# A hybrid decoder layer: sampled-value products written to four groups of output partitions by page number

## What is computed

```python
k_past = cache_k[l, page_table].reshape(db, past, N_HEADS, HEAD_DIM)
v_past = cache_v[l, page_table].reshape(db, past, N_HEADS, HEAD_DIM)
s = einsum('bqhd,bkhd->bhqk', q, k) * HEAD_DIM ** -0.5 + c_q - c_k
p = softmax(s)
o = einsum('bhqk,bkhd->bqhd', p, v)
```

## Time and profile before

| what | value |
|---|---|
| median of 3 runs | 3033.57 us (3032.75 to 3034.82) |
| the profiled execution's own time | 3031.26 us |
| its span, first to last instruction | 3029.5 us |
| mean granted TensorE clock | 0.968 |
| TensorE matmuls busy | 2848.4 us (94%) |
| VectorE busy | 1490.4 us (49%) |
| ScalarE busy | 718.6 us (24%) |
| DMA moved | 516.15 MB, mean 170 GB/s |

### The profile page before, as it was taken

One profiled execution on the slowest core, in us unless ns is written; L12 is line 12 of the kernel. 1 busy time (PEld: TensorE's weight loads), 2 busy tenths in 40 slices (PEclk: granted clock), 3 DMA queues, 4 the chain that ended last, 5 costly groups with the idle time before them and its releaser, 6 DMA issues.

```text
span 3029.5 us, 51183 instructions
## 1 busy us (share of the span) xinstructions
PE 2848.4 (94%) x19952; PEld 2399.5 (79%) x19952; DVE 1490.4 (49%) x5784; ACT 718.6 (24%) x949; POOL 18.1 (1%) x57
## 2 busy tenths in 40 slices
PE   6977999999999977699899999999999999999998
PEld 4964546546545424499899999999999999999998
DVE  6367566566566347643534344343434344343433
ACT  5321101101101026622322222222222222222221
POOL 1000000000000000000000000000000000000000
PEclk8988999999999988799999999999999999999999
DMA  6468898898898863233132232223223222322321
GB/s 216 138 229 326 319 378 335 325 378 331 331 378 328 314 208 105 82 98 113 56 112 84 84 111 85 84 96 101 84 84 110 86 84 95 101 84 84 109 87 60
DMA packets 265863, 516.15 MB, mean 170 GB/s; under 512 B 14162, under 2 KB 171435, under 8 KB 265076
## 3 DMA queue, kind: packets, MB, share of 16 engines
q1 hardware_dynamic: 257828, 496.26, 46.0%
q10 hardware_dynamic: 5760, 10.49, 0.9%
q0 software_dynamic: 2032, 6.13, 0.5%
HBM read 489.24 MB, written 24.02 MB: 169 GB/s over the span
## 4 chain that ended last, share of the span: by engine, by line
PE 58%; DVE 3%; ACT 2%; issue 1%; DVEq 0%; ACTq 0%
PE ps L624 57%; DVE t_work L1333 1%; PE ps L627 0%; DVE t_rmax L1650 0%; DVE t_aux L1590 0%; DVE t_aux L1333 0%; ACT t_aux L1196 0%; ACT L1196 0%; ACT L1198 0%; ACT t_aux L1198 0%; DVE t_work L342 0%; ACT t_work L1226 0%; DVE t_work L1598 0%; ACT t_wh L1021 0%; ACT L1061 0%
## 5 line engine op out<-in xcount | busy, mean ns | idle before, releaser
L624 PE MATMUL ps<-t_xh,t_wh 128*128 128x260 f32 x4608 | 943.4, 286 | 17.9 <-ACT t_work L1061 8.0
L624 PE MATMUL ps<-t_xh,t_wl 128*128 128x260 f32 x4608 | 934.5, 285 | 0.0
L624 PE MATMUL ps<-t_xl,t_wh 128*128 128x260 f32 x4608 | 933.3, 284 | 0.0
L1333 DVE TENSOR_TENSOR t_wl<-t_wraw,t_wh 128x1024 fp32r<-128x1024 f32 x376 | 459.8, 1224 | 867.6 <-ACT t_wh L1021 867.3
L1021 ACT ACTIVATE t_wh<-t_wraw 128x1024 fp32r<-128x1024 f32 x376 | 398.1, 1060 | 1907.0 <-PE ps L624 1906.0
L624 PEld LDWEIGHTS ps<-t_xh,t_wh 128*128 128x128 f32 x4608 | 717.0, 190 | 65.0 <-issue 44.3
L624 PEld LDWEIGHTS ps<-t_xh,t_wl 128*128 128x128 f32 x4608 | 716.8, 190 | 0.0
L624 PEld LDWEIGHTS ps<-t_xl,t_wh 128*128 128x128 f32 x4608 | 716.1, 190 | 0.0
L1459 DVE CUSTOM_DVE_ANT_0 t_work<-t_r,t_work 128x128 f32<-128x128 f32 x2048 | 455.1, 286 | 218.2 <-DMA t_r<-in_cache_k 205.2
L624 PE MATMUL ps<-t_r,t_pr 128*8 128x512 f32 x1024 | 456.3, 596 | 30.0 <-DMA t_r<-in_cache_v 28.7
L624 PEld LDWEIGHTS ps<-t_r,t_pr 128*8 128x8 f32 x1024 | 85.3, 90 | 354.7 <-issue 282.0
(11 more groups left out here) (186 smaller groups left out, 1057.1 us busy)
## 6 DMA issues: line engine op xcount, KB each, us to landing
t_r<-in_cache_k SPq DMA_DIRECT2D x256, 512.0 KB, 7.2
t_r<-in_cache_v SPq DMA_DIRECT2D x256, 512.0 KB, 6.8
t_wraw<-in_w_up SPq DMA_DIRECT2D x44, 2048.0 KB, 8.0
t_wraw<-in_w_down SPq DMA_DIRECT2D x22, 2048.0 KB, 7.9
t_wraw<-in_w_in SPq DMA_DIRECT2D x20, 2048.0 KB, 9.5
t_wraw<-in_w_o SPq DMA_DIRECT2D x8, 2048.0 KB, 9.9
scr_proj<-t_stg ACTq DMA_DIRECT2D x40, 256.0 KB, 3.9
t_aux<-scr_proj SPq DMA_DIRECT2D x12, 768.0 KB, 4.7
```

What stands on the lines that cost most here:

```text
L624: return pe.matmul(out, lhsT, rhs, start=start, stop=stop)
L1333: return dve.tensor_tensor(out, in0, in1, op)
```

## The change

Value page p is written to PSUM partitions 32 * (p % 4) to 32 * (p % 4) + 7 instead of always 0 to 7. Each of the four groups begins its own sum with its first page (p < 4) and ends it with its last (p >= 28). The order of the pages, chunks, waits and counts stays. At the end of a round ScalarE copies all 128 partitions, and the eight small matmuls take 128 rows instead of 8, against `quad`, a 128 by 8 array with a one wherever the partition is m modulo 32, so that the four groups are added there. VectorE makes `quad` and clears banks 4 and 5 once, before round 0; TensorE waits for that.

```diff
+        quad = sb("quad", [P, HEADS])
...
-        osb = work[0:HEADS, 7168:8192]
+        osb = work[:, 7168:8192]
...
-        o_rows, o_cols, o_kept = sems("o_rows_ready o_columns_full o_columns_kept")
+        o_rows, o_cols, o_kept, o_zero = sems("o_rows_ready o_columns_full o_columns_kept o_rows_zeroed")
...
             def value_page(r, p):
                 pe.wait_ge(v_loaded[p % RING], r * (16 * PAGES // RING) + 16 * (p // RING + 1))
+                lane = 32 * (p % 4)
                 for c in range(2):
-                    last = mm(ps[0:HEADS, 4 + c, :], pr[:, p, :], vring[:, p % RING, c * 512:(c + 1) * 512],
-                              p == 0, p == PAGES - 1)
+                    last = mm(ps[lane:lane + HEADS, 4 + c, :], pr[:, p, :], vring[:, p % RING, c * 512:(c + 1) * 512],
+                              p < 4, p >= PAGES - 4)
                 last.then_inc(v_used, 1)
...
                     for h in range(HEADS):
-                        last = mm(ps[:, 7, 144 + h:145 + h], osb[:, h * P:(h + 1) * P], ident[0:HEADS, h:h + 1])
+                        last = mm(ps[:, 7, 144 + h:145 + h], osb[:, h * P:(h + 1) * P], quad[:, h:h + 1])
...
             broadcast_q(0, 1)
+            pe.wait_ge(o_zero, 1)
             round_(0, True, True, False)
...
-                                copy(osb.rearrange("p (c n) -> p c n", c=2), ps[0:HEADS, 4:6, :]).then_inc(o_rows, 1)
+                                copy(osb.rearrange("p (c n) -> p c n", c=2), ps[:, 4:6, :]).then_inc(o_rows, 1)
...
             dve.wait_ge(e_kept, 4)
+            dve.tensor_reduce(quad[:, :], ident[:, :].rearrange("p (j m) -> p m j", j=4)[:, 0:HEADS, :], AX.X, ALU.add)
+            dve.memset(ps[:, 4:6, :], 0.0).then_inc(o_zero, 1)
```

## The result

The changed kernel takes 3014.96 us (median of 4 runs, 3011.51 to 3017.69) against 3034.2 us before: a ratio of 0.9936, 95% interval 0.9919 to 0.9953, or 19 us less. I had forecast 54 us less. The sign was right and the size was not: the time lies inside my wide range, but at little more than a third of the forecast gain, and outside the forecast's own range of 2965 to 3000.

A forecast was written before the change was run, and what follows sets the result against it. TensorE's matmuls were taken as the first limit, the DMA close behind. Seven rounds -48, round 8 -7, set-up +1.3 gave -54 us, so 2980 us; range 2957 to 3036, the forecast's own 2965 to 3000.

The forecast's parts named there:

- What bounded the kernel before: Rounds 1 to 7: TensorE first, busy 760.6 of 786.6 us, the DMA close behind at a share of 0.91.
- Overlap of the page matmuls: Value bursts: only neighbouring pages' last and first matmuls overlap, saving 10.7 us per round on TensorE if all pages have landed.
- 13 places of 16: Burst of four value pages, matmuls starting and ending in program order: 13 places in line instead of 16, 1.29 us less.
- What the landed pages allow: Bursts of five: fifth page lands about 4 us after issue, so some 0.8 of 1.72 us gained; 7.1 us per round altogether.
- overlap, but lateness eats it: Rival: fifth page lands 5 us or more after issue, bursts of five stay 8.7 us, clock falls; 3020 us, chance 0.06.
- Bursts of four: Three bursts of four value pages per round, each 1.29 us shorter.
- The DMA from the other side: DMA's round: floor 94.4 us, plus 1.4 for weight loads, plus a lull of 8 to 9; sum 104 to 106 us.
- the other sum: TensorE's side of a round: 3 x 1.29 + 4 x 0.8 = 7.1 us less; both sides agree on about 105.5 us.
- Round 8: Last round, value pages without keys: 7 us gained, bounds 2 and 10.
- Set-up and copies: Before round 0, quad and clear cost 1.3 us once; ScalarE's 128-row copy and the 128-row small matmuls cost zero.
- The clock: TensorE idling 5 to 10% more costs nothing; 14 us kept in the range for half speed at round ends.

The follow-up runs named there:

- ring5_before: A fifth value buffer added to the kernel before, without the groups: 3002.2 us, ratio 0.9903, rounds of 108.5 us.
- two_groups: The change with value pages alternating between two groups of partitions instead of four: 3013.62 us, ratio 0.9937, rounds of 109.1 us.
- ring5: The change with a fifth value buffer, in place of VectorE's scrap array: 2993.21 us, ratio 0.9871, rounds of 106.4 us.
- one_group: The change with every page on partitions 0 to 7 again, its other parts kept: 3037.65 us, ratio 1.0011 against the kernel before.
- half_groups: The change with a page's two halves in two groups, odd and even pages in two pairs of groups: 3018.57 us, ratio 0.9958.
- best_g2: The change with two groups by page, a fifth value buffer, earlier first weights, and set-up before the query wait: 2964.43 us, ratio 0.9781.
- early_w: The change with each round's first 2 MB weight load issued just ahead of the fifth key page: 3004.39 us, ratio 0.9912.

## Why the prediction was wrong

**What bounded the kernel before: right, and half the truth.** TensorE's line is the first limit: 108.5 us per round when never kept waiting (ring5_before). The second limit was to be the DMA's full rate. It was the ring, in the fourth and fifth bursts, and in the others the time at which the loads behind the lull and the weights are issued and land.

**Overlap of the page matmuls: the mechanism right, the size too small.** I had assumed program order and 13 places of 16. The rows show 1.92 us for 16, four side by side. This error was to the kernel's favour and did not matter, as two_groups shows: with half the overlap the time is the same.

**What the landed pages allow: the step that failed.** I had seen that the fifth page's buffer comes free only with the burst's first page, and then wrote that the page lands about 4 us after issue and that 0.8 us are gained per burst of five. In the burst shown it takes 5.07 us, and the burst is 9.0 us instead of 8.75: nothing is gained. From the earlier trace rows I had read "within 4.8 us" and taken 4, below my only evidence, where the row said no more than that it was hardly late. Over the rounds it is 4.9 us in the mean. With 5 us the chain of that step gives no gain for four bursts of seven, and by the table they gain 0.4 us per round together, where the term said 3.2. The chain is not all of it: ring5 shortens the fourth and fifth bursts but not the third and the sixth. The sixth took 12.6 us before, 3.6 of them waiting for pages, and I had counted it as one more burst of 8.75 us. I had "overlap, but lateness eats it", 3020 us, as the last rival, at a chance of 0.06. It is near the result partly by luck: it counts more for the bursts of four than they gave, and takes off 14 us for a clock that did not fall at the rounds' ends.

**Bursts of four.** I counted 1.29 us for each of three, 3.9 us per round; they gave 2.1 (table). The first gained 5.1 us and the second lost 5.4, since its first page comes behind the round's first weights and the lull. In the round shown TensorE waited 3.31 us for a page, and the next three took 7.58 us, with the clock at 0.66 from 605 to 613 us (the line of the windows above). The pages set that length and not the matmuls: in rounds 2 to 7 the burst ends 25.8 to 26.6 us after the exponentials, and in two_groups, where it starts 2.2 us later and has less to wait, 25.6 to 26.8 us. From the round's exponentials to the third burst it is 32.5 us in both kernels (621.09 less 588.59 after, 624.85 less 592.21 before, 32.6). What stayed is the last burst, 4.6 us instead of 7.0: three of its pages had landed, and it waits 0.7 us in the mean for the fourth.

**The DMA from the other side: the check that did not check.** I added the lull to the full rate and got 104 to 106 us, and took the agreement with the other sum as support. That sum assumed that the mid-round dips would go. ring5 has exactly that, with 106.4 us; the change has 296 and 274 GB/s in the dips and 109.7 us. Both sums rested on the same unshown step, that SyncE would no longer wait for TensorE. It waits 19.2 us in the round shown, instead of 22.9 before, and 14.9 us for VectorE, instead of 12.7.

**Round 8** gave 5 us of matmuls, and 3 us until the last convolution tile, where I had 7. **Set-up and copies**: clear and reduce were right at 1.2 us of the 1.3; the 3.3 us of one_group, with its interval of 0.6 to 6.4, do not contradict it. **The clock** I had costed at nothing. In the change that holds nearly (0.98 over the rounds instead of 0.99), but not in its second burst, and half_groups, with 0.84, gives back what it gains. At the rounds' ends, for which I had kept 14 us, the change is no worse: the first burst starts 6.7 us behind the exponentials in rounds 2 to 7 before, and in the change 5.2 us behind them in three of these and up to 6.7 in the others (clock 0.57 from 592 to 596 us before, 1.00 from 588 to 592 in the change).

**Left open.** From the first dense matmuls after the attention to the end the changed kernel took 1755.7 us in its profiled execution and the kernel before 1751.4, though the change touches nothing there; best_g2 and ring5 have 1753.9 and 1754.1. Single executions differ by that, and I leave it at that. The landing time of 5.07 us was not varied by itself: ring5 takes away the need to wait for it in the fourth and fifth bursts, which shows that the round trip was the limit there, not how its 14.9 us divide. What would shorten the second, third and sixth bursts was tried only by early_w's edit, and there for the first load of weights alone.

## What to carry to other kernels

Where an engine works in bursts from a ring of buffers, the time of a burst that needs more pages than the ring holds is at least a round trip: first page freed, load issued, landed, used. Work that becomes faster inside it is not gained; count the chain with the landing time that a row shows, before the sum of busy times. Two limits that agree on a number are support only if they do not share the assumption in question, here that the queue would stop waiting. And when work leaves a nearly full engine, look first for what it will wait for next: here one more buffer, made out of a scrap array, was worth more than matmuls of landed pages in a fourth of the time, and both together more than either.

## What was not expected of the hardware

Four float32 value pages with 8 output rows each, in four groups of 32 output partitions, ran side by side in full: 16 matmuls in 1.92 us against 7.03 us, while a single group's matmuls stay 0.43 us apart. All matmuls of one page stood ahead of the next page's in program order, and that did not hold the next page back: a later group's matmuls start beside an earlier group's first ones. ring5 shows the order, since the page in its fifth buffer has a tile name of its own, `t_work`. Here that page is the burst's second:

```profile
690.62 0.60 PE L635 MATMUL ps<-t_work,t_pr 128*8 128x512 f32 x1
690.63 1.00 PE L635 MATMUL ps<-t_r,t_pr 128*8 128x512 f32 x3
691.05 0.59 PE L635 MATMUL ps<-t_work,t_pr 128*8 128x512 f32 x1
```

Its second matmul starts at 691.05, behind the first one of a page that comes after it, at 690.63. The Trainium skill (TensorE: Matmul & The Clock Gate, Packing small matmuls) says that matmuls start and end in program order, and gives 2.38 times for three groups. By the order alone 13 places of 16 were to be expected, 5.7 us; the rows show 1.92.

Taking work from TensorE can lower its clock: in half_groups, with pages of 1.03 us and waits of 1.5 us between them, the granted clock over the rounds went from 0.98 to 0.84, and part of a chunk between the bursts ran at 1.2 GHz.
